# Expert gates: for one group of tokens in four, GpSimd subtracts the row numbers and ACT takes the absolute value over 512 columns

## What is computed

```python
best_s, pos = lax.top_k(cand_s, PEER_TOPK)
best_i = jnp.take_along_axis(cand_i, pos, axis=-1)
g = jax.nn.softmax(best_s, axis=-1)
...
a = jnp.einsum('cd,ced->ce', hc, u[ic])
a = jax.nn.gelu(a, approximate=False) * gc.astype(hc.dtype)
return jnp.einsum('ce,ced->cd', a, v[ic])
```

## Time and profile before

| | us |
|---|---|
| median of 3 runs | 2301.36 |
| lowest, highest | 2301.24, 2305.37 |
| time of the profiled run | 2300.44 |
| its span | 2298.5 |
| the stage of the gates, in that span | about 776 to 901 |

### The profile page before, as it was taken

One profiled execution on the slowest core, in us unless ns is written; L12 is line 12 of the kernel. 1 busy time (PEld: TensorE's weight loads), 2 busy tenths in 40 slices (PEclk: granted clock), 3 DMA queues, 4 the chain that ended last, 5 costly groups with the idle time before them and its releaser, 6 DMA issues. The chain is left out here.

```text
span 2298.5 us, 44104 instructions
## 1 busy us (share of the span) xinstructions
PE 2000.2 (87%) x15796; PEld 1924.2 (84%) x15796; DVE 1529.0 (67%) x3133; ACT 1222.9 (53%) x2399; POOL 15.3 (1%) x21
## 2 busy tenths in 40 slices
PE   6898878999999767999999973896998968799896
PEld 6887878999999656999999863896998967699896
DVE  5666555999655687666665657755687567567855
ACT  4454544767755797555556354002555543555554
POOL 0000000000000000000000000000000001100000
PEclk9999988999999999999999986886999989799998
DMA  5432423455565201555554430001464524045451
GB/s 177 149 99 93 130 92 110 165 174 178 179 199 193 83 0 46 192 192 192 192 194 161 151 97 19 1 1 53 157 196 160 173 75 129 5 160 190 152 179 65
DMA packets 96223, 295.96 MB, mean 129 GB/s; under 512 B 9315, under 2 KB 25830, under 8 KB 95974
## 3 DMA queue, kind: packets, MB, share of 16 engines
q1 hardware_dynamic: 96102, 294.35, 39.1%
HBM read 293.26 MB, written 1.05 MB: 128 GB/s over the span
## 5 line engine op out<-in xcount | busy, mean ns | idle before, releaser
L401 PE MATMUL bank<-a_high,w_high 128*128 128x256 f32 x3256 | 939.6, 289 | 141.4 <-DVE a_low L792 61.8
L375 DVE TENSOR_TENSOR w_low<-ring,w_high 128x512 fp32r<-128x512 f32 x1102 | 747.6, 689 | 427.5 <-ACT w_high L369 420.9
L369 ACT ACTIVATE w_high<-ring 128x512 fp32r<-128x512 f32 x1102 | 679.2, 628 | 461.2 <-PE bank L403 458.1
L402 PE MATMUL bank<-a_low,w_high 128*128 128x256 f32 x3256 | 923.2, 284 | 0.0
L403 PE MATMUL bank<-a_high,w_low 128*128 128x256 f32 x3256 | 922.7, 283 | 0.0
L401 PEld LDWEIGHTS bank<-a_high,w_high 128*128 128x128 f32 x3256 | 632.7, 194 | 158.3 <-issue 101.0
L402 PEld LDWEIGHTS bank<-a_low,w_high 128*128 128x128 f32 x3256 | 633.0, 194 | 0.4
L403 PEld LDWEIGHTS bank<-a_high,w_low 128*128 128x128 f32 x3256 | 633.1, 194 | 0.0
L401 PE MATMUL bank<-s_high,w_high 128*128 128x256 f32 x1024 | 283.5, 277 | 2.0 <-DVE s_low L1958 2.0
L402 PE MATMUL bank<-s_low,w_high 128*128 128x256 f32 x1024 | 283.4, 277 | 0.0
L403 PE MATMUL bank<-s_high,w_low 128*128 128x256 f32 x1024 | 283.3, 277 | 0.0
(11 more groups left out here) (324 smaller groups left out, 2034.9 us busy)
## 6 DMA issues: line engine op xcount, KB each, us to landing
ring<-in_stream SPq DMA_DIRECT2D x279, 512.0 KB, 3.5
ring<-in_peer_u SPq DMA_DIRECT2D x128, 512.0 KB, 3.4
ring<-in_peer_v SPq DMA_DIRECT2D x128, 512.0 KB, 3.4
ring<-in_stream SPq DMA_DIRECT2D x32, 256.0 KB, 3.2
x<-in_x SPq DMA_DIRECT2D x4, 256.0 KB, 5.2
arena<-in_mem SPq DMA_DIRECT2D x1, 1024.0 KB, 11.7
out<-x SPq DMA_DIRECT2D x4, 256.0 KB, 2.5
consts<-in_consts SPq DMA_DIRECT2D x1, 640.0 KB, 8.5
```

The lines of the kernel that those rows point to most:

```text
L369: self.nc.scalar.activation(self.w_high[:, h % SLOTS, :], self.raw(h), ACT.Copy)\
L375: self.nc.vector.tensor_tensor(self.w_low[:, h % SLOTS, :], self.raw(h), self.w_high[:, h % SLOTS, :].bitcast(F32), ALU.subtract)\
L401: self.nc.tensor.matmul(to, lh, rh, start=start, stop=False, **more)
L402: self.nc.tensor.matmul(to, lh, rl, start=False, stop=False, **more)
```

## The change

In `subtract`, batch 3 of every turn takes another way. POOL waits until `make` of batch 1 has read slot 1 of `distance`. It then writes iota - number for the batch's four tokens into that slot with one instruction over 512 columns, and signals `taken` (numbers_taken). ACT waits for `left` as before and then for `taken`, and takes the absolute value of the 512 columns in place with one instruction. It then goes on to `make` of batch 2. The four instructions at L1813 stay for batches 0, 1 and 2.

```diff
+        taken, apart, left, right, crossed, merged = (
+            self.counter(s) for s in ("numbers_taken", "numbers_apart", "left_made", "right_made",
+                                     "rows_crossed", "merged"))
...
                 def subtract(it, b):
                     if later(it) or b >= 2:
                         act.wait_ge(left.sem, it * step + left.at(b - 1))
+                    if b == step - 1:
+                        act.wait_ge(taken.sem, it + taken.at(1))
+                        nc.scalar.activation(distance[:, b % 2, :, :], distance[:, b % 2, :, :],
+                                             ACT.Abs).then_inc(apart.sem, 1)
+                        return
                     for i in range(batch):
...
+            @block.gpsimd
+            def _(pool):
+                with pool.Fori(0, turns) as it:
+                    pool.wait_ge(left.sem, it * step + left.at(2))
+                    numbers = turned[:, 0, bass.ds(it * each + (step - 1) * batch, batch)]
+                    nc.gpsimd.tensor_tensor(distance[:, 1, :, :],
+                                            iota.unsqueeze(1).broadcast_to([P, batch, N_KEYS]),
+                                            numbers.unsqueeze(2).broadcast_to([P, batch, N_KEYS]),
+                                            ALU.subtract).then_inc(taken.sem, 1)
...
+        taken.total += turns
```

More of the change, by code:

```diff
@@ L1790, in _ @@
                 ins.then_inc(spun.up(), 1)
-        apart, left, right, crossed, merged = (
-            self.counter(s) for s in ("numbers_apart", "left_made", "right_made", "rows_crossed",
-                                     "merged"))
+        taken, apart, left, right, crossed, merged = (
+            self.counter(s) for s in ("numbers_taken", "numbers_apart", "left_made", "right_made",
+                                     "rows_crossed", "merged"))
         scores = self.arena[:, 0:N_KEYS * T].rearrange("p (j t) -> p j t", t=T)
```

## The result

The changed kernel took 2304.47 us (median of 20 runs, 2291.66 to 2318.48), the kernel before, now with 20 runs, 2292.04 us (2282.24 to 2305.37). The ratio is **1.0045 (95% interval 1.0024 to 1.0067)**, some 10 us more (the two medians alone differ by 12.4). The direction and the mechanism of the forecast held. Its size, +15.4 us, was half as much again too large. The measured time lies 12.3 us under the forecast of 2316.8 and outside the range, 2306 to 2333, mainly because the three runs it started from, at 2301 us, lie at the upper end of the 20.

What follows compares the result with a forecast made beforehand. ACT was taken to set the pace, PE and DVE following; 0.25 + 1.40 + 0.10 + 0.52 - 1.32 = +0.95 us a turn, +1.05 in first and last, together +15.4 on 2301.36 gave 2316.8 us, range 2306 to 2333.

Steps and rivals of the forecast that it cites:

- The chain: In the gates' stage ACT sets the pace at 7.73 us a turn; PE and DVE follow it.
- A: On ACT, from the absolute value's start until batch 2's relu can start: 0.52 us a turn.
- H1: From the end of batch 1's relu on ACT to POOL's start: 0.25 us, 0.2 to 0.4 kept.
- H2: From the end of POOL's subtraction back to ACT: 0.10 us a turn.
- G: POOL's subtraction over 512 columns: 1.40 us, as two undisturbed 256-column instructions; low end 0.73, high end 1.91.
- Contention: POOL against DVE's SBUF instructions: DVE may lose 1.4 us a turn at no cost, or POOL up to 0.34 us.
- 1: POOL's step is longer than two quiet halves: 1.80 us a turn, 29 us for the kernel, 2330; chance 0.16.
- 2: The library's selection in POOL's loop is dear: at most 0.78 us more a turn, +12.5 us, 2329; chance 0.12.
- Rival 3: POOL's subtraction is short, 0.73 us, its start signal 0.2: +0.23 us a turn, 4 us, 2305; chance 0.07.
- Rival 4: POOL's subtraction is hidden by working ahead of ACT: -0.66 us a turn, -10.6 us, 2290.8; chance 0.02.
- the gap of 0.14 us: On ACT in the loop, between a relu's end and the next subtractions: wait for its own relu plus address computation.
- Rival C: From rerunning the changed kernel: clock or weight stream of other stages differs because of the change; no chance given.

Runs made afterwards that it cites:

- POOL aside: Kernel before, ACT keeping all its subtractions, plus POOL's 16 subtractions into unused columns with nobody waiting: ratio 1.0000 (0.9975 to 1.0025) to the kernel before, stage 125.4 us.
- slot of its own: Changed kernel with POOL writing to 512 unused columns, able to start ahead of ACT's need: ratios to the kernel before 0.9967 and, again, 0.9926; stage 112.8 and 112.7 us.

## Why the prediction was right and wrong

**The chain.** Right. ACT sets the stage, and the detour has nothing beside it: 8.25 to 8.33 us a turn all through the stage, POOL named at 16 of 16 waits, doubling POOL's work adds all of it, taking the wait away gives all of it back.

**A and H1.** Right: 0.54 us for 0.52, 0.26 for 0.25. The parts of H1 were off, 0.08 + 0.11 + 0.07 for 0.13 + 0.10 + 0.02; that their sum came out was luck, a signal too dear against a library too cheap.

**H2.** 0.03 us in place of 0.10, 1 us too much over 16 turns. The row it came from is of another pair, POOL to DVE, with POOL's next instruction already running; whether that made the 0.07 us isn't shown.

**G, the term that was mis-sized.** 1.04 to 1.10 us, mean 1.055, in place of 1.40: 0.35 x 16 = 5.5 of the 5.8 us by which the sum, +15.4, was above the stage's +9.6 (H2 adds 1.1, and A and H1 take 0.5 back). The step of the sum that failed is "since the same 512 columns go through in them". Two instructions of 256 columns pay the fixed 0.19 us twice; they overlap by 0.04, and the rest is the 0.14 between 1.40 and the plain 1.26. The form with the repeated numbers takes another 0.22 off. The prediction named the fixed part as a reason for less ("If part of an instruction's 0.73 is fixed, G is less") and then counted none. The Trainium skill has a figure from which one can be had. By "GPSIMD Engine Reference", section "3.1 Elementwise — side-by-side cycle accounting", 4497 ns over 2048 columns is 2.2 ns a column; the plain instructions here show 2.1 and 0.19 fixed, so the trace agrees. The 12 us that the prediction worked out from it was nearer to the 9.6 than its own sum, though 1.2 us isn't what G was.

**Contention.** Right in kind, and in that it cost nothing here; its size was put too high, a whole G a turn where DVE lost 7.0 us in the stage (77.9 against 70.9), 0.44 a turn. None of it reached ACT, as the kernel with POOL aside shows apart. It is free only while DVE has time to spare: the kernel with three more POOL instructions a turn is 11.2 us slower in the stage. The longest L1862 was 1064 ns, about one POOL instruction, against 348 before. The Trainium skill, "SBUF — State Buffer", section "Who interferes with whom", says the second one is blocked until the first has ended; the traces agree, here with DVE as the one that mostly waits: POOL's own 16 instructions took 1.04 in the median and 1.10 at most.

**The rivals.** 1 and 2 are refuted (G near 1.05; the library costs 0.07 us a turn, and its first call no more than the later ones, since the first of the 16 idle times on ACT is 1.4 us as the last). Rival 3, 2305, was the nearest in time, by luck: its +4 us stood on a level 9 us too high. (Its chance was given as 0.07, and then as 0.06 together with the low tail; the two don't fit.) Rival 4 can't happen in this kernel, and is what the slot of its own makes true; its price, -0.66 us a turn, was too small, -0.90 measured, because the gap of 0.14 us goes too and ACT's next instruction starts before the one ahead has ended.

**The level, the step that took the time out of the range.** The step is "on the median, 2301.36 + 15.4". The same sum on 2292.04, the median of 20 runs, is 2307.4, and the measured 2304.47 lies 3 us from it. So of the 12.3 us between forecast and result 9.3 are the level and 3.0 the sum; read as a difference, the range is +4.6 to +31.6 us, and the measured 10 to 12 us lie inside it in spite of G. The range carried the bounds of every term and nothing for the level, because three runs within 4 us looked firm. They are the first three of the 20. The next two took 2303.55 and 2298.44 us, and the fifteen after them have a median of 2291.1. In three later series of 33, 21 and 15 runs the kernel before had medians of 2294.8, 2293.3 and 2293.6. So three runs taken together don't show the spread.

What moves the level stays open. A part of it is seen ahead of the gates, in the same code in both kernels. Stretches of the kernel before, then of the changed one (us, PE busy, granted clock as a mean over the stretch, DMA share, GB/s):

```profile
0.00:776.00 776.00, 700.54 (x5406) 0.96 0.46 149
```

```profile
0.00:766.60 766.60, 690.49 (x5406) 0.98 0.47 151
```

The same 5406 matmuls, 10 us more of busy PE at a granted clock of 0.96 than at 0.98. Over all traces this part took 764 to 782 us, with 0.98 in the two shortest and 0.96 or 0.97 in the others. But the clock isn't the whole of it: over the 69 later executions of the kernel before, at 2283 to 2312 us with mean clocks of 0.927 to 0.940, the two go together only weakly (correlation -0.26). Rival C of the experiments rests on it: in both traces of the changed kernel that part was 9 to 12 us shorter than in the profiled one of before. But it lies ahead of the change, and with the same code there the kernel with POOL's loop written out took 777 us and the one with POOL aside 782. The ratios speak against it too: 1.0045 and 1.0041 agree, within their intervals, with what the stage alone gives, 9.6 of 2292 us or 0.42%. So I count it as spread; two traces don't prove it. In the stage of the gates itself the mean granted clock was 0.90 before and 0.83 after, and within the changed stage stretches of 14 us had from 0.76 to 0.98, while ACT's turn stayed within 8.25 to 8.33.

## What to carry to other kernels

Work that is handed to an idle engine is free only if that engine can start before the busy one needs it. Look at the buffer it writes to: if the last reader of that buffer is the instruction right ahead of the wait, the whole detour is added to the path; here nearly the same edit, with 512 unused columns to write to, went from +9.6 to -12.5 us. And look at whom the idle engine holds up: that costs nothing only as long as that engine has time to spare. Forecast a difference, with the level's own spread beside it, not a time built on a few runs.

## What the runs showed that I had not expected

- A GpSimd instruction of two inputs took 0.19 us and 2.1 ns a column; where the second input repeats the same element in a row, 1.67 ns a column (1.04 for 1.26 us over 512). The same row read again and again gave nothing. That the repetition is the reason, and not that the inputs lie in two tensors, isn't shown.
- The compiled program selects POOL's library ahead of the first instruction that needs it, and if that stands in a loop, in every turn: 32 entries of 11 ns, and 0.07 us a turn on a path. One POOL instruction written out ahead of the loop took it out.
- With registers for addresses, POOL answered ACT's signal in 0.19 us, with constants in 0.08.
